# Where the split activations begin, modulo 1024 bytes, behind the weights they are multiplied with

## The reference, cut to what matters

```python
D_MODEL = 1024; SEQ = 256; D_FF = 2816; D_FF_2 = 4 * D_MODEL
def swiglu_ffn(x, w_in, w_down):
    gate, up = jnp.split(x @ w_in, 2, axis=-1)
    return (jax.nn.silu(gate) * up) @ w_down
for i in range(DEPTH):                     # DEPTH = 2
    h = rwkv7_time_mix(x, ...) if i % 2 == 0 else moba_attention(x, moba_w_qkv[j], moba_w_o[j])
    x = layer_norm(ALPHA * x + h, ln_mix_g[i], ln_mix_b[i])
    x = layer_norm(ALPHA * x + swiglu_ffn(x, ffn_w_in[i], ffn_w_down[i]), ln_ffn_g[i], ln_ffn_b[i])
# third layer: projections of rmsnorm(x), cross attention to mem, relu(x @ w_ff1)^2 @ w_ff2
```

## The kernel before, in words

| norm q | products that read it | wide_fm slabs | wide_tm slabs |
|---|---|---|---|
| 0 | feed-forward part 0 (`ffn0`) | 22 | |
| 1 | queries, keys, values of the block attention | 8 | 4 |
| 2 | feed-forward part 1 (`ffn1`) | 22 | |
| 4 | mLSTM and forgetting attention, and the small gate product | 8 | 6 |
| 5 | keys and values of the memory | 4 | 4 |
| 6 | queries of the cross attention | 4 | |
| 7 | last feed-forward part (`ff2`) | 16 | |

## Time and profile before

### The profile page before, as it was taken

One profiled execution on the slowest core, in us unless ns is written; L12 is line 12 of the kernel. 1 busy time (PEld: TensorE's weight loads), 2 busy tenths in 40 slices (PEclk: granted clock), 3 DMA queues, 4 the chain that ended last, 5 costly groups with the idle time before them and its releaser, 6 DMA issues.

```text
span 1168.6 us, 24785 instructions
## 1 busy us (share of the span) xinstructions
PE 1141.0 (98%) x10550; PEld 1042.4 (89%) x10550; DVE 752.2 (64%) x1087; ACT 623.9 (53%) x916; POOL 119.5 (10%) x97
## 2 busy tenths in 40 slices
PE   7999999999999999999999999999999999999997
PEld 7798877789999989988999999899998898999996
DVE  7888886375554467897645445898587555555554
ACT  8974654454433446565634433675566564544443
POOL 0032263401100000220010000011000000000000
PEclk9999999999999999999999999999999999999999
DMA  8631111145554644434555447455434443655550
GB/s 302 226 108 48 55 57 56 61 163 195 195 195 157 244 180 174 151 109 145 180 217 188 179 172 252 147 178 197 164 129 148 158 144 126 217 188 178 211 179 36
DMA packets 29804, 187.30 MB, mean 160 GB/s; under 512 B 3472, under 2 KB 5648, under 8 KB 8592
## 3 DMA queue, kind: packets, MB, share of 16 engines
q1 hardware_dynamic: 27072, 177.21, 42.0%
q10 hardware_dynamic: 2640, 8.75, 2.3%
HBM read 184.90 MB, written 1.05 MB: 159 GB/s over the span
## 4 chain that ended last, share of the span: by engine, by line
PE 87%; DVE 6%; ACT 4%; issue 2%; DMA 0%; ACTq 0%; DVEq 0%; SPq 0%
PE ps L2125 25%; PE ps L2126 24%; PE ps L2127 24%; PE ps L2458 1%; PE ps L2453 1%; PE ps L2599 1%; PE ps L2262 1%; ACT mixed L639 1%; PE ps L2455 1%; DVE w_lo L1396 1%; PE ps L2347 1%; PE ps L2395 1%; PE ps L2846 1%; PE ps L2854 1%; ACT w_hi L745 1%
## 5 line engine op out<-in xcount | busy, mean ns | idle before, releaser
L1400 DVE TENSOR_TENSOR w_lo<-w_raw,w_hi 128x2048 fp32r<-128x2048 f32 x149 | 346.7, 2343 | 125.3 <-ACT w_hi L610 124.6
L2125 PE MATMUL ps<-x_hi,w_hi 128*128 128x256 f32 x1344 | 378.7, 282 | 4.3 <-DVE x_lo L1689 1.5
L2126 PE MATMUL ps<-x_lo,w_hi 128*128 128x256 f32 x1344 | 375.4, 279 | 0.0
L2127 PE MATMUL ps<-x_hi,w_lo 128*128 128x256 f32 x1344 | 375.2, 279 | 0.0
L610 ACT CAST w_hi<-w_raw 128x2048 fp32r<-128x2048 f32 x147 | 280.1, 1907 | 147.6 <-PE ps L2127 147.2
L2125 PEld LDWEIGHTS ps<-x_hi,w_hi 128*128 128x128 f32 x1344 | 252.8, 188 | 11.1 <-issue 4.7
L2126 PEld LDWEIGHTS ps<-x_lo,w_hi 128*128 128x128 f32 x1344 | 252.9, 188 | 1.3
L2127 PEld LDWEIGHTS ps<-x_hi,w_lo 128*128 128x128 f32 x1344 | 252.9, 188 | 0.0
L2125 PE MATMUL ps<-w_hi,hid_hi 128*128 128x512 f32 x304 | 118.8, 391 | 0.1
L2126 PE MATMUL ps<-w_lo,hid_hi 128*128 128x512 f32 x304 | 118.8, 391 | 0.0
L2127 PE MATMUL ps<-w_hi,hid_lo 128*128 128x512 f32 x304 | 118.4, 389 | 0.0
(11 more groups left out here) (419 smaller groups left out, 1782.3 us busy)
## 6 DMA issues: line engine op xcount, KB each, us to landing
w_raw<-in_weights SPq DMA_DIRECT2D x163, 1024.0 KB, 4.9
xt<-in_xT SPq DMA_DIRECT2D x2, 512.0 KB, 5.4
w_raw<-in_weights SPq DMA_DIRECT2D x2, 512.0 KB, 6.2
x_tm<-in_x SPq DMA_DIRECT2D x1, 1024.0 KB, 5.4
gain<-in_mix_g ACTq DMA_DIRECT2D x2, 512.0 KB, 5.1
gain<-in_mix_b ACTq DMA_DIRECT2D x2, 512.0 KB, 6.8
gain<-in_ffn_g ACTq DMA_DIRECT2D x2, 512.0 KB, 7.3
gain<-in_ffn_b ACTq DMA_DIRECT2D x2, 512.0 KB, 9.3
```

Of the source, the lines that this page charges most:

```text
L1400: V.tensor_tensor(w_lo[:, i % WS, :], w_raw[:, i % RAW, :], w_hi[:, i % WS, :].bitcast(F32), ALU.subtract).then_inc(lo_done, 1)
L2125: nc.tensor.matmul(out, hi_l, hi_r, start=start, stop=False)
L2126: nc.tensor.matmul(out, hi_l, lo_r, start=False, stop=False)
L2127: return nc.tensor.matmul(out, lo_l, hi_r, start=False, stop=stop)
```

## The change

`x_hi` and `x_lo` become 256 floats (1024 bytes) longer each, and so do `hid_hi` and `hid_lo`. In each stage the tile is laid into its buffer at another offset: `X_AT[q]` gives that of x_hi and that of x_lo in floats for norm q, `HID_AT[name]` those of hid_hi and hid_lo. Every write and read of the stage goes through the same view. To make room, three rows of scratch (`zf`, `za`, `ones_t`, 12 partitions each) now lie in `fx_k`, which is filled later. The instructions, their order on each engine, their shapes and their waits are the same in both programs; only addresses differ.

The buffer of x_hi still begins at 416 modulo 1024, and so does that of x_lo; those of hid still begin at 128. With offset n (floats) the distance is 288 + 4n for x and 4n for hid, modulo 1024 bytes:

| stage | x_hi, x_lo: distance in bytes | stage | hid_hi, hid_lo: distance in bytes |
|---|---|---|---|
| q = 0 (ffn0) | 16, 48 | ffn0 | 32, 16 |
| q = 1 | 8, 64 | ffn1 | 64, 48 |
| q = 2 (ffn1) | 288, 40 | ff2 | 8, 24 |
| q = 4 | 128, 96 | | |
| q = 5 | 192, 4 | | |
| q = 6 | 512, 256 | | |
| q = 7 (ff2) | 24, 56 | | |

```diff
+X_AT = {0: (188, 196), 1: (186, 200), 2: (0, 194), 4: (216, 208), 5: (232, 185), 6: (56, 248), 7: (190, 198)}
+HID_AT = {"ffn0": (8, 4), "ffn1": (16, 12), "ff2": (2, 6)}
...
-        x_hi = sb("x_hi", [P, KT, T], F32R, a_m)
-        x_lo = sb("x_lo", [P, KT, T], F32R, a_m)
+        x_hi, x_lo = (sb(n, [P, KT * T + 256], F32R, a_m) for n in ("x_hi", "x_lo"))
+
+        def hid_parts(name):
+
+            pair = []
+            for m, t in enumerate((hid_hi_a, hid_lo_a)):
+                n = HID_AT[name][m]
+                pair.append(t[:, n:n + 2 * 512].rearrange("p (a b) -> p a b", a=2))
+            return pair
+
+        def xh(q):
+            n = X_AT[q][0]
+            return x_hi[:, n:n + KT * T].rearrange("p (k c) -> p k c", k=KT)
...
-            hid_hi = sb("hid_hi", [P, 2, 512], F32R, a)
-            hid_lo = sb("hid_lo", [P, 2, 512], F32R, a)
+            hid_hi_a = sb("hid_hi", [P, 2 * 512 + 256], F32R, a)
+            hid_lo_a = sb("hid_lo", [P, 2 * 512 + 256], F32R, a)
...
-            zf, za, ones_t, gi = (sb(n, [12, T], where=a) for n in ("zf", "za", "ones_t", "gi"))
+            gi = sb("gi", [12, T], where=a)
+            zf, za, ones_t = (fx_k[0:12, n, :] for n in range(3))
...
-                V.tensor_tensor(x_lo[:, k:k + n, :], x_fm[:, k:k + n, :], x_hi[:, k:k + n, :].bitcast(F32), ALU.subtract)\
+                V.tensor_tensor(xl(q)[:, k:k + n, :], x_fm[:, k:k + n, :], xh(q)[:, k:k + n, :].bitcast(F32), ALU.subtract)\
...
-                                wide_fm(i, x_hi, x_lo, 4 + 2 * (j % 2) + m, r, slabs)
+                                wide_fm(i, xh(q), xl(q), 4 + 2 * (j % 2) + m, r, slabs)
```

More of the change, by code:

```diff
@@ L263, in build, with xl @@
         a_m = ctx.enter_context(ExitStack())
-        x_hi = sb("x_hi", [P, KT, T], F32R, a_m)
-        x_lo = sb("x_lo", [P, KT, T], F32R, a_m)
+        x_hi, x_lo = (sb(n, [P, KT * T + 256], F32R, a_m) for n in ("x_hi", "x_lo"))
[8 more added lines that the diff above has]
+            return x_hi[:, n:n + KT * T].rearrange("p (k c) -> p k c", k=KT)
+        def xl(q):
+            n = X_AT[q][1]
+            return x_lo[:, n:n + KT * T].rearrange("p (k c) -> p k c", k=KT)
         xn = sb("xn", [P, TT, C], where=a_m)
@@ L956, in to_features @@
                 if q not in BY_PARTS and q != 5:
-                    return nc.scalar.activation(x_hi[:, k, :], feature_tile(q, k), ACT.Copy, scale=pcol(g_at[0], g_at[1] + k))
+                    return nc.scalar.activation(xh(q)[:, k, :], feature_tile(q, k), ACT.Copy, scale=pcol(g_at[0], g_at[1] + k))
                 if q == 4:
@@ L964, in to_features, with high_part @@
                 return nc.scalar.activation(x_fm[:, k, :], feature_tile(q, k), ACT.Copy, scale=pcol(g_at[0], g_at[1] + k))
-            def high_part(k, n):
-                nc.scalar.copy(x_hi[:, k:k + n, :], x_fm[:, k:k + n, :]).then_inc(xhi_ready, n)
+            def high_part(q, k, n):
+                nc.scalar.copy(xh(q)[:, k:k + n, :], x_fm[:, k:k + n, :]).then_inc(xhi_ready, n)
             def features(q):
@@ L976, in features @@
                     link(to_features(q, k))
-                    high_part(k, 1)
+                    high_part(q, k, 1)
                 act.wait_ge(xfm_ready, 2 * FM_NORMS.index(q) + 1)
-                high_part(2, 2)
+                high_part(q, 2, 2)
                 to_features(q, 6)
                 link(to_features(q, 7))
-                high_part(6, 2)
+                high_part(q, 6, 2)
                 act.wait_ge(xfm_ready, 2 * FM_NORMS.index(q) + 2)
-                high_part(4, 2)
+                high_part(q, 4, 2)
             def late_squares(q):
@@ L1036, in ffn @@
                 s0, n, h0, per, rounds = FFN[name]
+                hid_hi, hid_lo = hid_parts(name)
                 slabs = per * (2 if name == "ff2" else 3)
@@ L1200, in _ @@
             for i in range(4):
-                high_part(2 * i, 2)
+                high_part(5, 2 * i, 2)
             take_scaled("fx_v", 1, fx_v)
@@ L1697, in features @@
                         dve.wait_ge(xhi_ready, KT * FM_NORMS.index(q) + 2 * (k // 2) + 2)
-                        V.scalar_tensor_tensor(x_lo[:, k, :], feature_tile(q, k), pcol(g_at[0], g_at[1] + k),
-                                               x_hi[:, k, :].bitcast(F32), ALU.mult, ALU.subtract).then_inc(xlo_ready, 1)
+                        V.scalar_tensor_tensor(xl(q)[:, k, :], feature_tile(q, k), pcol(g_at[0], g_at[1] + k),
+                                               xh(q)[:, k, :].bitcast(F32), ALU.mult, ALU.subtract).then_inc(xlo_ready, 1)
                     return
@@ L2564, in step @@
                             if j == 0 and m == 0:
-                                wide_as_ready(i, x_hi, x_lo, 4, k_order(q), xlo_ready, q if q == 7 else None)
+                                wide_as_ready(i, xh(q), xl(q), 4, k_order(q), xlo_ready, q if q == 7 else None)
                             else:
-                                wide_fm(i, x_hi, x_lo, 4 + 2 * (j % 2) + m, r, slabs)
+                                wide_fm(i, xh(q), xl(q), 4 + 2 * (j % 2) + m, r, slabs)
                     view = lambda w, j: w[:, (j - 1) % 2, :].rearrange("p (k n) -> p k n", k=2)
@@ L2589, in project @@
                     pe.wait_ge(p_taken, max(n - 2, P_FIRST["x_q"]) if n >= P_FIRST["x_q"] else n - 2)
+                q = 1 if n < P_FIRST["ml_qk"] else 4 if n < P_FIRST["x_k"] else 6
                 if order:
-                    wide_as_ready(i, x_hi, x_lo, n % 3, order, xlo_ready, late)
+                    wide_as_ready(i, xh(q), xl(q), n % 3, order, xlo_ready, late)
                 else:
-                    wide(i, x_hi, x_lo, n % 3)
+                    wide(i, xh(q), xl(q), n % 3)
             def p_transposes(u, s, kind):
@@ L2691, in gates @@
                 for k in range(KT):
-                    last = three(ps[0:36, 3, 0:T], gate_hi[:, k, :], gate_lo[:, k, :], x_hi[:, k, :], x_lo[:, k, :],
+                    last = three(ps[0:36, 3, 0:T], gate_hi[:, k, :], gate_lo[:, k, :], xh(4)[:, k, :], xl(4)[:, k, :],
                                  k == 0, k == KT - 1)
@@ L2705, in memory_product @@
                 if n == 0:
-                    wide_as_ready(memory_slab(0), x_hi, x_lo, MEMORY_BANK[0],
+                    wide_as_ready(memory_slab(0), xh(5), xl(5), MEMORY_BANK[0],
                                   [(k, KT * FM_NORMS.index(5) + 2 * (k // 2) + 2) for k in range(KT)], xlo_ready)
                 else:
-                    (wide_tm if n >= 4 else wide_fm)(memory_slab(n), x_hi, x_lo, MEMORY_BANK[n])
+                    (wide_tm if n >= 4 else wide_fm)(memory_slab(n), xh(5), xl(5), MEMORY_BANK[n])
             def row(n):
```

## The result

The changed kernel takes 1177.26 us (median of 4 runs, 1176.70 to 1178.63) against 1168.99 us (4 runs) before: ratio 1.0065, 95% interval 1.005 to 1.0081. It is slower by 8.3 us; 1158 was forecast. The profiled execution's span is 1175.8 us, 7.2 more than before, with the granted clock as high as before.

What follows compares the result with a forecast made beforehand. TensorE, busy 98% of the span, was taken to bound the kernel by matmuls times cadence. Terms -8.9 + 1.1 - 3.1 + 0 = -10.9 us gave 1158.3 us, with a range of 8 in 10 from 1143 to 1179.

Steps and rivals of the forecast that it cites:

- What bounds the kernel: Whole kernel: time is the number of matmuls times their cadence, TensorE busy 98% of the span; no new wait appears.
- That the distance counts: Dense products: cadence follows an address within a product, between about 113 and 120 ns.
- the price of near distances: x moving, 2624 matmuls at distances up to 64 bytes: 113.3 instead of 116.7 ns, -8.9 us.
- The picture behind the price: x moving: a tile beginning a few words behind the weights runs twice as fast and is not met again; -3.4 ns.
- hid: Tall slabs, hid stationary, 912 matmuls: -3.4 ns each, -3.1 us, bounds -9.9 to +3.1 us.
- x stationary: 672 matmuls with weights moving and x loaded: 0, between -3.2 and +1.3 us.
- The writes of the splits, the scratch rows: Split writes at unaligned words: 0, bound +1.5 us; scratch rows in fx_k, beside the projections: 0.
- The rival that came true in its number: ffn0 and ff2: near zero as dear as zero, cost highest at 0 and 512; +8.4 us, 1177.6 us, chance 0.26.
- The signs: ffn0 about 113 ns, ffn1 lines differing, 24 tall-slab matmuls 5.36 us, stages 4 and 6 117 to 120, rx 117.4.

Runs made afterwards that it cites:

- the weights' move: Changed kernel with all offsets zero and seven small buffers (288 bytes) declared ahead of w_raw: 1187.34 us in one run, +17.5 us.
- the last kernel: Changed kernel with x at 448 in all stages, hid at 464 in ffn0, 432 in ffn1, 32 and 16 in ff2: 1167.62 us, one run.
- everything at 448: Changed kernel with x and hid at distance 448 bytes in all stages: 1163.36 us (6 runs), ratio 0.9944 to the kernel before.

## Why the prediction was wrong

- *What bounds the kernel* held: no wait of TensorE grew by more than 0.6 us (that for mix_lo, in the time mix), the one for x_lo stayed at 1.5 us, and the time moved by matmuls times cadence. Stage by stage the cadences give +5.5 us for x and +3.9 us for hid.
- *That the distance counts* held, and was shown by the weights' move: x goes to 120.0 ns where it stands, once it is at distance 0.
- *The step that failed* is the price of near distances: "Distances up to 64 bytes" were put at "the best that rows show, 113.3 instead of 116.7: -3.4 ns" for 2624 matmuls. Measured with equal distances they are 120.0 at 8, 118.7 at 16, 116.7 at 32, 118.4 at 48, 117.8 at 64: on average dearer than the 116.7 they replace. In the changed kernel stages 0, 1 and 7, priced at -7.5 us together, cost +2.4 us. The picture behind the price, two streams of which the faster one is ahead and so not met again, has no place for 8 bytes being as slow as 0. I had taken 113.3 from the gate product, at distances of 592 and 736 bytes and with 36 stationary columns, and carried it to near distances and 128 columns: neither was in the rows.
- *hid*, -3.1 us forecast, cost +3.9 us; forecast had its distance 0 as the dear one because x-like products are slow there. With 512 columns moving, 0 was among the best that were tried (227.6, and 226.7 beside x at 448; 256 gave 226.7 too), and the distances 8 to 64 cost 230.8 to 232.9 ns. What is a good distance depends on the count of moving columns: x stationary, which like hid has the weights moving but 256 columns of them, ran at 120.0 with distance 0 when the weights were moved.
- *x stationary*, priced at 0 between -3.2 and +1.3, came out at 0.0 as the sum of -0.3, +0.4 and -0.1 us.
- *The writes of the splits, the scratch rows*: 0, as forecast; the kernel with offsets zero has the scratch rows too.
- *The rival that came true in its number* (1177.6 us, measured 1177.26) did not in its mechanism: it had +3.0 us in ffn0, which won 1.3 us, and nothing for hid, which lost 3.9. Its curve, falling from 0 to 288, is not there.
- *The signs.* ffn0 stood at 115.6 ns, neither at 113 nor at 118 to 120, and behind the tall slabs only beside the moved hid. In ffn1 the steps that begin with L2146, in which x_lo moves, were 117.1 ns and the two others 118.3 and 118.5, where 113.3 and 116.7 were forecast. Stages 4 and 6 came to 118.6 and 119.8, as forecast. rx did not keep its 117.4 but ran at 118.7, though nothing of it was touched.
- That a cadence also depends on what ran just before was missing from the prediction, and the profile before had it. Two slabs ahead of the first tall slab of ffn0 take 11.30 us for 96 steps, 117.7 ns; behind it the same products take the 116.7 of the earlier trace rows:

```profile
262.90 0.28 PE L2125 MATMUL ps<-x_hi,w_hi 128*128 128x256 f32 x1
...
274.20 0.39 PE L2125 MATMUL ps<-w_hi,hid_hi 128*128 128x512 f32 x1
```

The tall slabs' first five steps, mostly at 228 to 236 ns before they settled at 226.7, are a hint of the same: the pattern seems to need time to lock. The earlier trace rows begin behind them, so their 226.5 ns is below the 227.6 of a whole tall slab.

What stays open: which property of the two streams makes 448 good and 440 bad. That steps fall into a repeating pattern is seen (in ffn0 of the changed kernel 119, 112 and 115 ns for the three matmuls of a product, over and over), and, with x at 448, that what follows a tall slab depends on hid: 448, (32, 16) and (64, 48) led to 113.3 to 113.9 ns (in the last kernel (32, 16) only after one slab at 117.8), 0, 256 and, after one slab at 113.9, 496 to 117.8, each in one traced execution. The cause inside TensorE or the memory was not measured, nor what decides a stretch's first entry. Which of two cadences a stage without tall slabs falls into could not be foretold: those stages (1, 4, 5, 6) went between 113.3 and 117.8 from slab to slab with everything at 448.

## What to carry to other kernels

When TensorE's steps (start to start) in a dense stretch without pauses exceed their columns by some 10 ns, compare the cadence of products of one shape whose operands begin at different addresses modulo 1024 bytes; 3 to 6% of a matmul stood in that alone. Do not reason the good distance out from a picture: scan it, several distances in one program, a stage each, in steps no wider than 8 bytes, since good ones are narrow. Then try the winner in the whole program, with its neighbours in time, because a stretch can be thrown into its slower pattern by the products that come before it, and the effects of two edits do not add. Judge it by several runs: the same instructions at the same addresses entered either pattern here.

## What the runs showed of the hardware

- The step of a 256-column matmul with a load of 128 columns for each lies between 113.3 and 120.2 ns, depending on the distance of the two operands modulo 512 bytes, at the full granted clock (2.4 GHz, 106.7 ns for the columns). For 512 columns it is 226.7 to 233.5 ns. Whether VectorE, ScalarE or the DMA worked beside the 256-column steps moved them by less than 0.3 ns in the three traces compared.
- It is the distance, not an operand's address: with the weights moved, x and mix, which begin 416 bytes into their 1024, run at 119.9 to 120.0 ns, the cadence of distance 0, and x had run at 116.7 from the same place.
- At some distances two cadences are possible, 113.3 or 117.8 ns at 448 bytes, and 115.6 or 117.8 ns for x_hi at 16 and x_lo at 48; either lasts over hundreds of matmuls. rx, at 672, ran at 117.3 or 118.7 ns with the same instructions and addresses ahead of it.
- Addresses alone, with the same instructions and counts on every engine, made this kernel take 1.5% longer (weights moved, one run) or 0.6% shorter (everything at 448, 0.3 to 0.7%).
